# A decoder layer on one core: sums of squares taken slice by slice, transposes per token tile, and two weight splits moved behind the norm or softmax

## What is computed

```
rmsnorm(x, g) = x * rsqrt(mean(x * x) + 1e-6) * g
h = rmsnorm(x, ln1_g);  z = h @ w_in
y_a = rmsnorm(sparse_attention(z), nsa_norm_g)     # 8 heads of 128 columns
y_b = rwkv7(z)
x = x + concat(y_a, y_b) @ w_out
x = x + memory_attention(rmsnorm(x, ln2_g), rmsnorm(mem, ln_mem_g))   # 4 heads, wq, wo: 2048x2048
x = x + hier_moe(rmsnorm(x, ln3_g))                # 4 groups of 8 experts
out = rmsnorm(x, lnf_g)
```

## Time and profile before

| | |
|---|---|
| three runs | 1944.14, 1943.70, 1938.69 us; median 1943.7 |
| the profiled execution | 1943.37 us, of which the span of the trace is 1941.5 |
| PE busy | 1774.4 us, 91% |
| DVE busy | 941.5 us, 48% |
| ACT busy | 665.9 us, 34% |
| granted PE clock, mean | 0.946 |
| loop 0, loop 1, loop 2 on PE | from 871.0, 987.8 and 1132.7 us |
| memory attention on PE | from 1082.6 us |

### The profile page before, as it was taken

How to read it: one execution, slowest core, us unless ns; L and a number is a source line. 1 busy time by engine, 2 the same in 40 slices (tenths; PEclk the granted TensorE clock), 3 DMA queues, 4 the chain that set the end, 5 groups by cost and what they waited for, 6 DMA issues and landing times.

```text
span 1941.5 us, 28278 instructions
## 1 busy us (share of the span) xinstructions
PE 1774.4 (91%) x11978; PEld 1526.5 (79%) x11978; DVE 941.5 (48%) x1119; ACT 665.9 (34%) x709; POOL 72.6 (4%) x150
## 2 busy tenths in 40 slices
PE   6999999999989999969879789669999999998993
PEld 4887878878788888869879689668877886886882
DVE  1142423434223111143443334448878878887883
ACT  1011111101111111132333323236765765765772
POOL 4010010101010000000000000000000000000000
PEclk9899999999969999989989999769999998999997
DMA  7430605133126444416525153239977987995972
GB/s 204 143 106 9 207 11 172 53 109 115 45 94 213 131 130 130 130 69 191 173 87 177 39 164 124 87 121 360 380 302 270 378 309 267 378 372 204 380 300 109
DMA packets 173374, 351.55 MB, mean 181 GB/s; under 512 B 12707, under 2 KB 145388, under 8 KB 147436
## 3 DMA queue, kind: packets, MB, share of 16 engines
q1 hardware_dynamic: 173292, 350.33, 51.4%
HBM read 348.22 MB, written 2.10 MB: 180 GB/s over the span
## 4 chain that ended last, share of the span: by engine, by line
PE 89%; DVE 4%; ACT 3%; issue 1%; POOL 1%; DMA 1%; SPq 0%; DVEq 0%; ACTq 0%; POOLq 0%
PE bank L683 20%; PE bank L1114 18%; PE bank L999 10%; PE bank L1133 9%; PE bank L672 7%; PE bank L1003 5%; PE bank L1079 2%; PE bank L898 1%; PE bank L787 1%; PE bank L704 1%; PE bank L802 1%; PE bank L1100 1%; PE bank L797 1%; PE bank L1037 1%; ACT split L1425 1%
## 5 line engine op out<-in xcount | busy, mean ns | idle before, releaser
L1878 DVE TENSOR_TENSOR split<-weights_raw,split 128x2048 fp32r<-128x2048 f32 x192 | 439.0, 2292 | 90.0 <-ACT split L1425 87.0
L683 PE MATMUL bank<-arena_fixed 128*128 128x256 f32 x1792 | 414.3, 386 | 0.0
L1425 ACT CAST split<-weights_raw 128x2048 fp32r<-128x2048 f32 x192 | 367.0, 1914 | 121.9 <-PE bank L1114 73.3
L683 PEld LDWEIGHTS bank<-arena_fixed 128*128 128x128 f32 x1792 | 334.9, 191 | 53.9 <-issue 8.3
L1114 PE MATMUL bank<-split,gathered_hi 128*128 128x512 f32 x1024 | 323.1, 397 | 13.8 <-DVE split L1878 9.3
L1114 PEld LDWEIGHTS bank<-split,gathered_hi 128*128 128x128 f32 x1024 | 191.3, 190 | 53.8 <-issue 10.0
L1114 PE MATMUL bank<-split,gathered_lo 128*128 128x512 f32 x512 | 201.8, 394 | 0.0
L999 PE MATMUL bank<-loop_split,act_over_hT 128*128 128x256 f32 x768 | 166.7, 286 | 7.7 <-DVE act_over_concat L1719 7.7
L1133 PE MATMUL bank<-split,hidden_hi 128*128 128x512 f32 x512 | 163.3, 401 | 5.3 <-DVE hidden_lo L1917 5.3
L999 PE MATMUL bank<-loop_split,act_over_concat 128*128 128x256 f32 x768 | 165.6, 285 | 2.8 <-DVE act_over_hT L1773 2.8
L1726 DVE TENSOR_TENSOR loop_split<-arena_fixed,loop_split 128x2048 fp32r<-128x2048 f32 x48 | 107.8, 2288 | 84.3 <-ACT loop_split L1354 84.3
(11 more groups left out here) (353 smaller groups left out, 1791.9 us busy)
## 6 DMA issues: line engine op xcount, KB each, us to landing
weights_raw<-in_moe_w_gate_dram SPq DMA_DIRECT2D x64, 1024.0 KB, 5.1
weights_raw<-in_moe_w_up_dram SPq DMA_DIRECT2D x64, 1024.0 KB, 7.1
weights_raw<-in_moe_w_down_dram SPq DMA_DIRECT2D x32, 2048.0 KB, 7.6
arena_fixed<-in_w_in_dram SPq DMA_DIRECT2D x22, 2048.0 KB, 8.2
arena_fixed<-in_wk_mem_dram SPq DMA_DIRECT2D x8, 2048.0 KB, 8.9
arena_fixed<-in_wv_mem_dram SPq DMA_DIRECT2D x8, 2048.0 KB, 8.6
arena_fixed<-in_w_out_dram SPq DMA_DIRECT2D x8, 2048.0 KB, 8.7
arena_fixed<-in_wq_mem_dram SPq DMA_DIRECT2D x8, 2048.0 KB, 8.6
```

Of the source, the lines that this page charges most:

```text
L683: mm = pe.matmul(b[:, half * T:half * T + T], w[:, c, half * P:half * P + P], hT[:, c, :], start=st, stop=en)
L1425: nc.scalar.copy(split_half(i, 0, j), raw_half(j, hf)).then_inc(act_hi, 1)
L1878: V.tensor_tensor(split_half(i, 1, j), raw_half(j, hf), split_half(i, 0, j).bitcast(F32), ALU.subtract)\
```

## The change

Four edits. (1) For na, n2 and n3 the squares are no longer taken by `sumsq`: ACT squares each head's output right after it is copied to `ya`, and in loops 0 and 2 each slice of `x` after its addition (`squares`), with an accumulator into a column of its own in `rms_p`; DVE adds the eight columns (`tensor_reduce`) before the mean. In those loops ACT's step waits for DVE's addition instead of for PE. (2) The scaling of each token tile signals by itself, and PE's transposes of tile 0 wait for tile 0 alone (n1, nm, na, n2, n3). (3) The last unit's splitting for the following loop, slot 1 (`loop_weights(NLU, 1)` and `loop_weights(2 * NLU, 1)`), leaves the last step of loops 0 and 1: the first now comes after n2's last group, the second after the output of head 1 on ACT and within head 2 on DVE. (4) The last pass of each loop is written out behind the loop, on ACT and DVE.

```diff
@@ -124,6 +124,7 @@
         rms_r = fixed.take(2)
+        rms_p = fixed.take(2, 8)
         gates = fixed.take(2, 24)
@@ -411,11 +412,13 @@
+        SUMMED = {"na": 16, "n2": 32, "n3": 48}
+        squared = sem("act_squared")
         NORMS = ("n1", "nm", "na", "n2", "n3")
         fills = {k: (4 if k == "na" else 8) for k in NORMS}
-        act_n = Progress(sem("act_norm"), [k for n in NORMS + ("nf",) for k in [(n, "sq"), (n, "sqrt")]])
+        act_n = Progress(sem("act_norm"), [k for n in NORMS + ("nf",) for k in ([] if n in SUMMED else [(n, "sq")]) + [(n, "sqrt")]])
         dve_n = Progress(sem("dve_norm"), [k for n in NORMS for k in
-                                           [(n, "var"), (n, "xn")] + [(n, "out", f) for f in range(fills[n])]]
+                                           [(n, "var"), (n, "xn", 0), (n, "xn", 1)] + [(n, "out", f) for f in range(fills[n])]]
                          + [("nf", "var"), ("nf", "out")])
@@ -694,9 +697,10 @@
             def norm_transposes(name, src, nf):
-                pe.wait_ge(*dve_n.at((name, "xn")))
                 for f in range(nf):
                     tt, c4 = divmod(f, nf // 2)
+                    if c4 == 0:
+                        pe.wait_ge(*dve_n.at((name, "xn", tt)))
                     if f >= 4:
@@ -1179,14 +1183,17 @@
+            def root(name):
+                act.wait_ge(*dve_n.at((name, "var")))
+                A(rms_s, rms_r, ACT.Sqrt).then_inc(*act_n.mark((name, "sqrt")))
+
             def sumsq(name, src, n, junk):
...
                 ins.then_inc(*act_n.mark((name, "sq")))
-                act.wait_ge(*dve_n.at((name, "var")))
-                A(rms_s, rms_r, ACT.Sqrt).then_inc(*act_n.mark((name, "sqrt")))
+                root(name)
@@ -1313,6 +1320,7 @@
             SC = HD ** -0.5
+            junk = flat(concatT)[:, 0:NT * NH * HD].rearrange("p (t d) -> p t d", t=NT)
             for i in range(NHT + 2):
@@ -1341,6 +1349,9 @@
                     nc.scalar.copy(ya[:, tt, h * P:h * P + P], bank[7][:, 0:P]).then_inc(*act_a.mark(("o", i - 2)))
+                    act.wait_ge(*act_a.at(("o", i - 2)))
+                    A(junk[:, tt, h * P:h * P + P], ya[:, tt, h * P:h * P + P], ACT.Square, accum_out=rms_p[:, tt, h:h + 1])\
+                        .then_inc(squared, 1)
                     gap2(FILL2)
@@ -1353,10 +1364,20 @@
+            def squares(i, s, n):
+
+                act.wait_ge(out_loop, n * NLU + s + 3 + 2 * i)
+                for tt in range(NT):
+                    A(xn[:, tt, bass.ds((2 * i + s) * UC, UC)], x[:, tt, bass.ds((2 * i + s) * UC, UC)], ACT.Square,
+                      accum_out=rms_p[:, tt, bass.ds(2 * i + s, 1)]).then_inc(squared, 1)
+
             def loop_stream(n, out_copy=False, last=False):
...
                 def step(i, s, weights):
-                    act.wait_ge(pe_loop, 2 * i + n * NLU + s + 1)
+                    if out_copy:
+                        act.wait_ge(pe_loop, 2 * i + n * NLU + s + 1)
+                    else:
+                        squares(i, s, n)
                     if out_copy:
@@ -1365,24 +1386,26 @@
-                with act.Fori(0, NLU // 2 - int(last)) as i:
+                with act.Fori(0, NLU // 2 - 1) as i:
                     for s in range(2):
                         step(i, s, True)
+                step(NLU // 2 - 1, 0, not last)
+                step(NLU // 2 - 1, 1, False)
             activations_hi(over_hT, concatT, NC // 2, NC)
-            sumsq("na", ya, NH * HD, pr.rearrange("p a b -> p (a b)")[:, 0:NH * HD])
+            root("na")
             loop_weights(0, 0)
...
             loop_stream(0)
-            act.wait_ge(out_loop, 2 + NLU)
-            sumsq("n2", x, D, flat(hT)[:, 0:D])
+            root("n2")
             for f in range(8):
...
                 nc.scalar.copy(over_concat[o], hT[o]).then_inc(src_hi, 1)
+            loop_weights(NLU, 1)
             loop_stream(1, out_copy=True)
@@ -1398,10 +1421,11 @@
                 ins.then_inc(*act_m.mark(("o", h)))
+                if h == 1:
+                    loop_weights(2 * NLU, 1)
             loop_stream(2, last=True)
-            act.wait_ge(out_loop, 2 + 3 * NLU)
-            sumsq("n3", x, D, flat(hT)[:, 0:D])
-            act.wait_ge(*dve_n.at(("n3", "xn")))
+            root("n3")
+            act.wait_ge(*dve_n.at(("n3", "xn", 1)))
             nc.scalar.copy(h3[0][:, :, :], xn).then_inc(*act_r.mark("h3hi"))
@@ -1496,7 +1520,11 @@
-                dve.wait_ge(*act_n.at((name, "sq")))
+                if name in SUMMED:
+                    dve.wait_ge(squared, SUMMED[name])
+                    link(V.tensor_reduce(rms_s, rms_p, AX.X, ALU.add))
+                else:
+                    dve.wait_ge(*act_n.at((name, "sq")))
                 V.tensor_scalar(rms_r, rms_s, 1.0 / n, EPS, ALU.mult, ALU.add).then_inc(*dve_n.mark((name, "var")))
@@ -1509,6 +1537,8 @@
                                                      in1=order(gain), op0=ALU.mult, op1=ALU.mult)
+                    if name != "nf":
+                        ins.then_inc(*dve_n.mark((name, "xn", tt)))
                 return ins
@@ -1538,7 +1568,7 @@
                 .then_inc(*dve_c.mark("prm"))
-            norm("n1", x_slot, x_slot, D).then_inc(*dve_n.mark(("n1", "xn")))
+            norm("n1", x_slot, x_slot, D)
             norm_out("n1", hT, c_ln1)
@@ -1665,7 +1695,7 @@
-            norm("nm", mem_slot, mem_slot, D).then_inc(*dve_n.mark(("nm", "xn")))
+            norm("nm", mem_slot, mem_slot, D)
             dve.wait_ge(*act_proj.at(last_in))
@@ -1728,7 +1758,7 @@
             activations_lo(over_concat, concatT, over_hT, (everything, slice(NC // 2, NC), everything), 1)
-            norm("na", ya, ya, NH * HD).then_inc(*dve_n.mark(("na", "xn")))
+            norm("na", ya, ya, NH * HD)
             norm_out("na", concatT, c_nsa)
@@ -1747,16 +1777,15 @@
-                with dve.Fori(0, NLU // 2 - int(last)) as i:
+                with dve.Fori(0, NLU // 2 - 1) as i:
                     for s in range(2):
                         step(i, s, True)
-                if last:
-                    for s in range(2):
-                        step(NLU // 2 - 1, s, False)
+                step(NLU // 2 - 1, 0, not last)
+                step(NLU // 2 - 1, 1, False)
...
             loop_stream(0)
-            norm("n2", x, xn, D).then_inc(*dve_n.mark(("n2", "xn")))
+            norm("n2", x, xn, D)
@@ -1786,10 +1816,12 @@
                     output_lo(h - 1)
+                if h == 2:
+                    loop_weights(2 * NLU, 1)
             output_lo(MH - 1)
...
             dve.wait_ge(s_late, 80)
-            norm("n3", x, xn, D, gain=lnb, order=by_partition).then_inc(*dve_n.mark(("n3", "xn")))
+            norm("n3", x, xn, D, gain=lnb, order=by_partition)
             norm_out("n3", hT, None)
             V.tensor_tensor(h3[1][:, :, :], xn, h3[0][:, :, :].bitcast(F32), ALU.subtract).then_inc(*dve_r.mark("h3lo"))
```

## The result

| | before | after |
|---|---|---|
| median (lowest to highest, runs) | 1945.68 us (1938.69 to 1948.33, 6) | 1928.24 us (1924.84 to 1931.69, 6) |
| ratio to before | | 0.9915, 95% interval 0.9896 to 0.9934 |
| profiled execution, span | 1943.37, 1941.5 | 1926.0, 1924.1 |
| granted clock, mean | 0.946 | 0.952 |

The change makes the kernel 17.4 us faster by the medians and by the spans alike. The forecast was 1924.4, in a range of 1920 to 1931. Most terms came out as forecast; one lost more than was forecast (head 2 of the attention), and one gain had no term.

A forecast was written before the change was run, and what follows sets the result against it. TensorE (PE) was taken to bound the kernel, at 89% of the chain that ended last. Gains of 1.3 + 1.1 + 6.9 + 4.4 + 5.3 = 19.0 us took 1943.37 to 1924.4, range 1920 to 1931.

The forecast's parts named there:

- n1: Normalisation before the first projection: transposes start after one tile's scaling, half of 2.68; gain 1.3 us, 0 to 1.4.
- na: Normalisation between sparse attention and loop 0: squares and table load leave the path; gain 1.1 us, 0.5 to 1.4.
- n2: Normalisation between loops 0 and 1: only two slice squares remain, splits move behind; gain 6.9 us, 6.0 to 7.5.
- n3: Normalisation between loop 2 and router: shorter squares, tile 0 transposed during tile 1's scaling; gain 5.3 us, 4.0 to 6.2.
- The attention: Memory attention, loop 1 to loop 2: head 0 gains 3.4 and 2.1, head 2 loses 1.1; gain 4.4 us, 1.8 to 4.9.
- 3.4 + 2.1: Attention head 0: 3.4 us from no longer waiting for DVE's subtractions, 2.1 from value matmuls at the full clock.
- I take head 0's row, so no fall: Attention head 2: pause grows to 3.0 us, but head 0's clock fell only 4.0 us after PE's last matmul.
- Rival 1: Clock falls at attention head 2, costing 2.5 us, also covering other restarts met a little worse; 1926.9 us, chance 0.22.
- Loops 0 to 2: Casts and subtractions in loops 0 and 2 come later but stay hidden; loops no longer, gain 0.
- The cover: Loops 0 and 2: first half's subtraction done at 6.2 us, PE needs it at 11.5; cover 5 us.
- rival 4: Slower: squares lengthen every step of loops 0 and 2, each needing to be 3.7 us dearer; 1949.4 us, chance 0.03.
- Rival 3: Gain handed back downstream, where later stages wait for something independent of PE; 1938 to 1949 us, chance 0.04.

The follow-up runs named there:

- casts_in_gap: Against the changed kernel, ACT's two casts for loop 2 moved ahead of head 1's output copies in the memory attention; 1928.10 us, ratio 0.9919.
- transposes_wait_tile_1: Against the changed kernel, PE's transposes wait for the scaling of both token tiles again, as before the change; 1936.95 us, ratio 0.9967.
- the next kernel: casts_in_gap plus a root of an unused column before loop 2's last step, loading the root's table early; 1926.07 us, ratio 0.9911.

## Why the prediction was right, and where not

**n1** (1.3 forecast, 1.03): right in the mechanism; PE starts after one tile's scaling (1.34 of 2.73), but the scaling itself began 0.33 later than in the earlier trace rows, behind an input that landed at 8.75, ahead of which this part of the kernel has nothing changed.

**na** (1.1, 1.42): right in both parts. The reason that I gave, the cast and the subtraction of the activations as the last to hand over, is what the chain shows. The squares were cheaper than the 0.5 I had taken: 0.40 with the read.

**n2** (6.9, 6.94): right, and the experiments show that the sum was rightly made as one path and not part by part. Squares of 128x256 cost 0.92 for the pair with both reads (1.1 taken from the exponential's row); the added reduction was 0.18 for the 0.2 taken.

**n3** (5.3, 4.94): the mechanism right, two sizes a little off. The scaling took 7.51, 0.3 more than in the earlier trace rows, and PE resumed only 0.88 after DVE's first copy had begun and then ran its last four groups at the half clock (3.66).

**The attention** (4.4, 2.9): this is the step that failed. Its first part, head 0, came out: 10.66 us from the first score to the end of the first value products against 16.13, so 5.5 for 3.4 + 2.1. The casts cost 0.93 at head 2 for 1.1. But "I take head 0's row, so no fall" was wrong. Rival 1 happened and cost 1.69, for 2.5 priced. And the reasoning of both was off: I compared the time from PE's last matmul to a fall or to the end of a pause (4.0 us at head 0, 2.1 at n2, 3.0 and 1.9 here) as if one length decided. The casts_in_gap run has only pauses of 1.9 and 0.7, and the clock falls all the same, at head 3; other kernels had it at head 1, or at 1 and 2, or 0 and 3, and in transposes_wait_tile_1 not at head 2 in spite of its pause of 2.82. What they share is that PE waits in every head, 1.9 us behind the scores and 0.7 behind the transposes; with these waits filled no head was slow. The Trainium skill (TensorE: Matmul & The Clock Gate, The HAM clock gate) says that the activity window is free-running, so that the same work meets it at another phase; the runs agree as far as they go, since unchanged heads are slow in one kernel (head 1 with 5.41) and not in another (3.73). The one kernel that was profiled twice had its fall at head 2 both times, so a change from run to run is not shown. From the runs alone: of the eleven profiles without filler, the one before included, seven have one slow head and four have two; none has none. One fall costs 1.7 to 2.2 in the value products. So a forecast for any version with these waits has to count at least one fall, and head 0's 2.1 as gained only in part. What decides between the heads was not found.

**Loops 0 to 2** (0 forecast, −0.61, −0.39, 0): no step became longer. The differences are all in the first microseconds, at the half clock. They were put in rival 1 as "other restarts met by the clock a little worse", and the filled kernels show what the restarts cost in all: 2.5 at loop 0 and 1.95 at loop 1. The cover, however, was wrong: I wrote 5 us, and the ring leaves 3.3. By the same mistake rival 4 had its point too far out. Each step is late by the full excess beyond 3.3, in each unit: to undo 19 us and lose 6 over 12 steps the squares would have to cost 5.4 us more per step, that is 2.7 each and not 3.7.

**The router** (no term, +1.45): its 64 products of 36 columns run partly at the half clock in both kernels, and how many do varies: they took from 10.17 to 12.96 us in the kernels run here, with no edit to them. That is the clock again, this time to the good, and no part of the change. It hides as much as the attention fell short, so that the total came within 1.6 of the forecast is in part luck.

The sum forecast was 19.0, and 17.4 came. Rival 3 did not happen: of the 17.68 gained when the expert stage's first gather begins, 17.4 are left at the end.

## What to carry to other kernels

When a stage of several engines is shortened, write down each engine's own order of work in it and ask which comes second; here the slice sums were worth nothing until DVE's subtractions had moved as well. A step inside a loop has as much cover as the last wait in its ring of engines, which is one number in brackets in the timeline (3.3 us here), not the distance from one product to its user. And where TensorE waits often, filler can pay: transposes of the identity into an unused bank through the waits, sized to end with them, gave about 5 us more here by the medians (1920.97 against 1926.07, with intervals that overlap; 1919.18 with three waits more filled, clear of it). Look at the waits left unfilled as well: with filler in the attention alone, loop 2 took back 1.5 of the 1.7.

## What was not expected of the hardware

- The clock can fall in a stretch whose longest pause is 1.9 us: value products of 5.41 instead of 3.72 at head 3 of casts_in_gap, and at head 1 of the next kernel. And it can stay up over a pause of 2.82 (head 2 of transposes_wait_tile_1, 3.72).
- With the waits of all four heads filled, the restart at the next unfilled wait was dearer: loop 2 at 93.90 for 92.43. That the one brought about the other is not shown.
- The router's 64 products of 128x36 follow each other without a gap, and still the granted clock goes from 0.92 (1231 to 1233 in the kernel after) to 0.50 (1233 to 1235) and stays there to 1241.
- A table load of 1.28 us that was moved off the path brought the root forward by 0.80 and no more, since DVE's mean was ready only 0.83 before the load's end.
